# Differential attention on one core: the two maps are combined one tile further ahead, half on VectorE and half on GpSimd, with four buffers of scores

## The chip, the core and the metric

The kernel is one program on one core of a Trainium2 chip. Its engines are TensorE (PE), VectorE (DVE), ScalarE (ACT), GpSimd (POOL) and the queue that issues DMAs (SP). The metric is the time of one launch in device microseconds: the median of several runs, lower is better.

## What is computed

A two-layer decoder step: a gated linear attention layer, then a differential attention layer, both for a prompt of 2048 rows and for 64 sample rows. The change is in the prompt part of differential attention. There are 8 heads of 128 columns; each head has two maps of 64 columns:

```python
s = jnp.einsum('bqhmd,bkhmd->bhmqk', qs, ks).astype(F32) * (DIFF_DH ** -0.5)
s = s + bias[None, :, None]
s = jnp.where(rel >= 0, s, jnp.finfo(F32).min)
p = jax.nn.softmax(s, axis=-1)
a = p[:, :, 0] - lam * p[:, :, 1]
return jnp.einsum('bhqk,bkhd->bqhd', a, v.astype(F32))
```

## The kernel before

The phases run one after another with a barrier between them: projection, recurrence, residual, projection, prompt attention, sample attention, residual. Only `attention` is changed. It runs over 8 heads H and, in each, over T = 16 tiles i of 128 queries; tile i has i+1 blocks of 128 keys (the causal part). The loop over heads is unrolled by two; inside a head all 16 tiles are written out. Every engine has its own program of the same shape, and semaphores tie them together. No scheduler is involved: the order on each engine is the order in which the code is written.

What is done for tile i, by function:

- `scores` (PE, L1661 to L1665): for each piece of up to 512 keys and each of the two maps three matmuls into one of RING = 4 PSUM banks `ps_s`. Two maps of one piece of keys take two banks, called a chunk below: tiles 0 to 3 have one chunk, 4 to 7 two, 8 to 11 three, 12 to 15 four. The first chunk of a tile is the one that is cut short. A bank is written again only after `take` has read it (`piece_free`).
- `take` (DVE, L1819 and L1826): adds the bias, writes the scores to `s_sb` in SBUF and keeps the maxima; at its end L1834 and L1836 make the negated maximum `neg`.
- `exps` (ACT, L1741): the exponential of the whole row in place, once for each map m, with the row's sum into `total`.
- `combine` (DVE, L1844 to L1852): the reciprocals `inv`, a weight for the second map, and `a = s[1] * weight + s[0]` over all (i+1)*128 columns.
- `turn` (PE, L1678) transposes `a` in groups of four blocks into the banks `ps_a`; `copies` (ACT, L1753) moves a group to SBUF as `a_t`; `meet` (PE, L1692) multiplies it with v into `ps_o`; `output` (ACT, L1760) scales and writes the tile's result, and counts `o_copied`.
- `prep`, `high`, `low` (L1643, L1735, L1793 and L1796) prepare q and k of the next head, one eighth in every even tile.

In iteration i the engines do this: PE the scores of tile i+2, with turns and meets of tile i woven in after the second chunk; ACT `exps(i+1, 0)`, then the first two copies of tile i, then `exps(i+1, 1)`, the other copies, `output(i)`; DVE `take(i+1)`, then `combine(i)`. GpSimd does nothing in this phase.

Of the kernel before, what the change touches and what calls it, by code (L numbers as in the profile page):

```python
# [11 lines left out]
ALU = mybir.AluOpType  # L12
# [3 lines left out]
P = 128  # L16
# [36 lines left out]
class Core:  # L53


    def __init__(self, nc, ctx):
        self.nc, self.ctx, self.sems = nc, ctx, []

        self.passed = {e.engine: nc.alloc_semaphore(name=f"passed_{i}")
                       for i, e in enumerate((nc.vector, nc.tensor, nc.sync))}  # L60
# [1439 lines left out]
def attention(core, q, k, v, rev, rel_bias, o):  # L1500
# [14 lines left out]
    RING = 4  # L1515

# [3 lines left out]
    with ExitStack() as mem:  # L1520
# [3 lines left out]
        def ps(name):  # L1524
# [12 lines left out]
        s_sb = [sb(f"s{i}", [P, 2, SEQ]) for i in range(2)]  # L1537
# [7 lines left out]
        weight = sb("weight", [P, 1])  # L1545
# [11 lines left out]
              "weight_done a_done a_turned a_copied a_met o_copied").split()}  # L1557
# [4 lines left out]
        def ahead(H, u, i, by):  # L1562

            return (H, u, i + by) if i + by < T else (H + 1, 1 - u, i + by - T)

# [13 lines left out]
        with nc.Block() as block:  # L1579
# [53 lines left out]
            def _(pe):  # L1633
# [35 lines left out]
                def turn(H, i, g):  # L1669

                    if g == 0:
                        pe.wait_ge(s["a_done"], after(T * H + i + 1))
# [52 lines left out]
                for i in range(2):  # L1725
                    for _ in scores(0, 0, i):
                        pass
# [3 lines left out]
            def _(act):  # L1731
# [6 lines left out]
                def exps(H, u, i, m):  # L1738
                    n = (i + 1) * P
                    act.wait_ge(s["neg_done"], after(T * H + i + 1))  # L1740
                    nc.scalar.activation(s_sb[i % 2][:, m, 0:n], s_sb[i % 2][:, m, 0:n], ACT.Exp,  # L1741
                                         bias=neg[i % 2][:, m:m + 1],
                                         accum_out=total[i % 2][:, m:m + 1]).then_inc(s["exp_done"], 1)
# [40 lines left out]

            @block.vector
            def _(dve):
# [13 lines left out]
                def take(H, u, i):  # L1800
# [3 lines left out]
                    if not (isinstance(H, int) and H == 0 and i == 0):  # L1804

                        dve.wait_ge(s["a_done"], after(T * H + i - 1))
# [3 lines left out]
                    for c, (lo_, hi_) in enumerate(pieces[i]):  # L1810
                        cut, start = min(hi_, near), max(lo_, near)
                        for m in range(2):
# [5 lines left out]
                            if cut > lo_:  # L1818
                                ins = nc.vector.tensor_scalar(s_sb[i % 2][:, m, lo_:cut],  # L1819
# [3 lines left out]
                            if hi_ > near:  # L1823
                                if cut <= lo_:
                                    stand_alone(dve, core)
                                ins = nc.vector.tensor_tensor_reduce(  # L1826
                                    out=s_sb[i % 2][:, m, start:hi_], in0=ps_s[n % RING][:, start - lo_:hi_ - lo_],
# [10 lines left out]
                def combine(H, u, i):  # L1838
                    n = (i + 1) * P
                    dve.wait_ge(s["exp_done"], after(2 * (T * H + i + 1)))  # L1840
                    if i >= 2:

                        dve.wait_ge(s["o_copied"], after(T * H + i - 1))
# [3 lines left out]
                    nc.vector.scalar_tensor_tensor(weight[:, :], total[i % 2][:, 0:1], core.neg_lambda[:, :],  # L1847
# [3 lines left out]
                    dve.wait_ge(s["a_turned"], after(GROUPS * H + first_group[max(i - 1, 0)]))  # L1851
                    nc.vector.scalar_tensor_tensor(a[i % 2][:, 0:n], s_sb[i % 2][:, 1, 0:n], weight[:, :],  # L1852
                                                   s_sb[i % 2][:, 0, 0:n], ALU.mult, ALU.add).then_inc(s["a_done"], 1)
# [10 lines left out]
                dve.sem_inc(s["piece_free"], RING)  # L1864
                for n, (is_q, g) in enumerate(preps):
                    low(0, 0, n, is_q, g, turn_banks)
                take(0, 0, 0)
                over_heads(dve, head)
# [507 lines left out]
```

## Time and profile before

| | |
|---|---|
| median of 3 runs | 3785.05 us (3784.03 to 3786.7) |
| profiled execution, its time | 3788.77 us |
| its span | 3787.0 us |
| PE, DVE, ACT, POOL busy over the span | 3424.4, 1771.8, 1099.7, 118.9 us |
| mean granted TensorE clock | 0.959 |
| prompt attention | from about 2157 to 3022 us of the span |

Times in the profile are microseconds from the start of the span. "Idle before" stands for the time in which an engine stood still ahead of an instruction, and behind the arrow is what released it. A line such as `L1852` is a line of the kernel before. Busy times count overlapping instructions of an engine once.

### The profile page before, as it was taken

What the parts mean: (1) busy time and instruction counts of PE and PEld (TensorE: products, weight loads), DVE (VectorE), ACT (ScalarE), POOL (GpSimd) and SP (SyncE); (2) the same over time, 40 slices, a digit from 0 to 9 for tenths busy, and PEclk for the clock granted to TensorE, in tenths of its full rate; (3) what the DMA queues carried; (4) which work ended last, traced back from release to release, by engine and by line L of the source; (5) the groups of instructions that cost most, each with busy time, mean ns of one, the idle gap of its engine ahead of it and who ended that gap; (6) DMA issues with size and microseconds to landing.
All of it is one profiled execution on the core that took longest, in us unless ns stands there. A gap on an engine that the chain in (4) does not pass through costs nothing. (4 is left out here: it accounts for less than half of the span.)

```text
span 3787.0 us, 54465 instructions
## 1 busy us (share of the span) xinstructions
PE 3424.4 (90%) x19319; PEld 2764.8 (73%) x19319; DVE 1771.8 (47%) x4120; ACT 1099.7 (29%) x1875; POOL 118.9 (3%) x158
## 2 busy tenths in 40 slices
PE   9999997995999989999999888888888778589999
PEld 7888995773888868888888666666666645378887
DVE  2123113555555542111113388887888734455554
ACT  2111102332121212111111166666666522311111
POOL 0000002110000000000000000000000000000000
PEclk9999998997999999999999989999999988799999
DMA  4621213336222224122221311111110088622221
GB/s 169 87 79 64 81 48 103 116 103 227 87 78 84 77 78 137 70 73 73 77 78 60 93 43 46 41 46 41 45 40 12 15 316 311 232 85 76 89 76 48
DMA packets 199098, 350.72 MB, mean 93 GB/s; under 512 B 19005, under 2 KB 109918, under 8 KB 198894
## 3 DMA queue, kind: packets, MB, share of 16 engines
q1 hardware_dynamic: 198894, 348.04, 27.9%
q8 instruction: 123, 2.02, 0.2%
q14 instruction: 81, 0.66, 0.1%
HBM read 243.50 MB, written 104.47 MB: 92 GB/s over the span
## 5 line engine op out<-in xcount | busy, mean ns | idle before, releaser
L362 PE MATMUL in_ps_y<-in_w_hi,in_x_hi 128*128 128x512 f32 (+2 forms) x1920 | 725.3, 378 | 0.0
L366 PE MATMUL in_ps_y<-in_w_hi,in_x_lo 128*128 128x512 f32 (+2 forms) x1920 | 722.2, 376 | 0.0
L364 PE MATMUL in_ps_y<-in_w_lo,in_x_hi 128*128 128x512 f32 (+2 forms) x1920 | 722.1, 376 | 0.0
L366 PEld LDWEIGHTS in_ps_y<-in_w_hi,in_x_lo 128*128 128x128 f32 x1920 | 361.5, 188 | 60.4
L362 PEld LDWEIGHTS in_ps_y<-in_w_hi,in_x_hi 128*128 128x128 f32 x1920 | 361.8, 188 | 59.8 <-ACT in_out L437 0.6
L364 PEld LDWEIGHTS in_ps_y<-in_w_lo,in_x_hi 128*128 128x128 f32 x1920 | 361.7, 188 | 58.9
L506 DVE COPY in_out<-in_ps_y 128x512 f32<-128x512 f32 (+2 forms) x88 | 56.7, 645 | 686.2 <-PE in_ps_y L366 647.0
L1819 DVE TENSOR_SCALAR_CACHE_REDUCE att_s<-att_ps_s,att_far 128x256 f32<-128x256 f32 (+3 forms) x608 | 328.4, 582 | 43.5 <-PE att_ps_s L1665 35.4
L1692 PE MATMUL att_ps_o<-att_v,att_a_t 128*128 128x128 f32 x2176 | 305.6, 289 | 32.5 <-ACT att_a_t L1753 31.6
L1692 PEld LDWEIGHTS att_ps_o<-att_v,att_a_t 128*128 128x128 f32 x2176 | 268.7, 196 | 85.5 <-ACT att_a_t L1753 58.5
L1741 ACT ACTIVATE att_s<-att_s,att_neg 128x128 f32<-128x128 f32 (+15 forms) x256 | 306.8, 1199 | 7.7 <-DVE att_neg L1836 7.6
L437 ACT ACTIVATE in_out<-in_ps_y 128x512 f32<-128x512 f32 (+2 forms) x88 | 49.4, 561 | 678.7 <-PE in_ps_y L366 636.7
L1255 PE MATMUL res_ps_f<-res_w_hi,res_o_hi 128*128 128x512 f32 x544 | 221.1, 406 | 7.8 <-ACT res_w_hi L1367 7.8
L1678 PE MATMUL att_ps_a<-ident,att_a 128*128 128x128 f32 x1088 | 166.8, 284 | 66.5 <-DVE att_a L1852 65.4
L1255 PE MATMUL res_ps_g<-res_w_hi,res_h_hi 128*128 128x512 f32 x544 | 218.7, 402 | 3.9 <-issue 3.9
L1257 PE MATMUL res_ps_f<-res_w_lo,res_o_hi 128*128 128x512 f32 x544 | 217.9, 400 | 0.0
L1259 PE MATMUL res_ps_f<-res_w_hi,res_o_lo 128*128 128x512 f32 x544 | 217.6, 400 | 0.0
L1259 PE MATMUL res_ps_g<-res_w_hi,res_h_lo 128*128 128x512 f32 x544 | 215.8, 397 | 0.0
L1257 PE MATMUL res_ps_g<-res_w_lo,res_h_hi 128*128 128x512 f32 x544 | 215.7, 397 | 0.0
L1678 PEld LDWEIGHTS att_ps_a<-ident,att_a 128*128 128x128 f32 x1088 | 122.6, 143 | 118.3 <-DVE att_a L1852 107.6
L1753 ACT ACTIVATE att_a_t<-att_ps_a 128x512 f32<-128x512 f32 (+2 forms) x320 | 160.0, 532 | 152.4 <-PE att_ps_a L1678 151.4
L1852 DVE SCALAR_TENSOR_TENSOR att_a<-att_s,att_weight 128x128 f32<-128x128 f32 (+15 forms) x128 | 173.0, 1352 | 23.8 <-PE att_ps_a L1678 12.1
(256 smaller groups left out, 4792.4 us busy)
## 6 DMA issues: line engine op xcount, KB each, us to landing
smp_k_pg<-in_cache_k SPq DMA_DIRECT2D x64, 512.0 KB, 5.7
smp_v_pg<-in_cache_v SPq DMA_DIRECT2D x64, 512.0 KB
res_factors<-factors SPq DMA_DIRECT2D x34, 512.0 KB
res_o<-mixer_out SPq DMA_DIRECT2D x34, 512.0 KB, 4.5
factors<-in_out SPq DMA_DIRECT2D x64, 256.0 KB, 2.0
in_stage<-in_diff_w_in SPq DMA_DIRECT2D x16, 1024.0 KB, 8.5
gla_x<-gla_qka SPq DMA_DIRECT2D x17, 520.0 KB, 3.5
gla_v<-gla_v SPq DMA_DIRECT2D x17, 512.0 KB, 4.3
```

Of the source, the lines that this page charges most:

```text
L362: nc.tensor.matmul(bank[:, cols], x_hi[:, k, rows], w_hi[:, k, cols], start=(k == 0), stop=False)
L364: nc.tensor.matmul(bank[:, cols], x_hi[:, k, rows], w_lo[:, k, cols], start=False, stop=False)
L366: mm = nc.tensor.matmul(bank[:, cols], x_lo[:, k, rows], w_hi[:, k, cols], start=False, stop=(k == KD - 1))
L1255: nc.tensor.matmul(dst[:, cols], hi[kind][:, k, :], w_hi[n][:, k, cols], start=(k == 0), stop=False)
L1257: nc.tensor.matmul(dst[:, cols], hi[kind][:, k, :], w_lo[n][:, k, cols], start=False, stop=False)
L1259: mm = nc.tensor.matmul(dst[:, cols], lo[kind][:, k, :], w_hi[n][:, k, cols], start=False, stop=(k == K - 1))
L1678: mm = nc.tensor.transpose(ps_a[n % 2][:, (b % 4) * P:(b % 4 + 1) * P], a[i % 2][:, b * P:(b + 1) * P], core.ident[:, :])
L1692: mm = nc.tensor.matmul(ps_o[:, 0:D_VD], a_t[n % 2][:, (b % 4) * P:(b % 4 + 1) * P], v_sb[u][:, b, :], start=(b == 0), stop=(b == i))
L1741: nc.scalar.activation(s_sb[i % 2][:, m, 0:n], s_sb[i % 2][:, m, 0:n], ACT.Exp, bias=neg[i % 2][:, m:m + 1], accum_out=total[i % 2][:, m:m ...
L1753: nc.scalar.activation(a_t[n % 2][:, 0:cols], ps_a[n % 2][:, 0:cols], ACT.Copy).then_inc(s["a_copied"], 1)
L1819: ins = nc.vector.tensor_scalar(s_sb[i % 2][:, m, lo_:cut], ps_s[n % RING][:, 0:cut - lo_], far[u][:, :], None, ALU.add, ALU.max, accum_ou ...
L1852: nc.vector.scalar_tensor_tensor(a[i % 2][:, 0:n], s_sb[i % 2][:, 1, 0:n], weight[:, :], s_sb[i % 2][:, 0, 0:n], ALU.mult, ALU.add).then_i ...
```

## The change

`combine` is moved ahead by one tile on DVE: iteration i is now `take(i+2)`, then `combine(i+1)`, and `take(1)` and `combine(0)` stand ahead of the loop. PE's scores are made three tiles ahead instead of two (AHEAD = 3). There are four buffers `s_sb` instead of two, and two of `weight`. `combine` writes on DVE only the first i//2+1 blocks of `a` (`own`); the others are made on GpSimd by a `tensor_scalar` (times weight, in place) and a `tensor_tensor` (add). The program of ScalarE is the same except for the number of the buffer.

```diff
+    AHEAD, HELD = 3, 4
...
-        s_sb = [sb(f"s{i}", [P, 2, SEQ]) for i in range(2)]
+        s_sb = [sb(f"s{i}", [P, 2, SEQ]) for i in range(HELD)]
...
-                        if not (last and i + 2 >= T):
-                            ahead_to = ahead(H, u, i, 2)
+                        if not (last and i + AHEAD >= T):
+                            ahead_to = ahead(H, u, i, AHEAD)
...
+            @block.gpsimd
+            def _(pool):
+                def combine(H, u, i):
+
+                    cols = slice(own(i) * P, (i + 1) * P)
+                    if own(i) > i:
+                        return
+                    pool.wait_ge(s["weight_done"], after(T * H + i + 1))
+                    stand_alone(pool, core)
+                    nc.gpsimd.tensor_scalar(s_sb[i % HELD][:, 1, cols], s_sb[i % HELD][:, 1, cols],
+                                            weight[i % 2][:, :], None, ALU.mult).then_inc(s["a_weighed"], 1)
+                    wait_turned(pool, H, i)
+                    pool.wait_ge(s["a_weighed"], after(pooled(H, i)))
+                    nc.gpsimd.tensor_tensor(a[i % 2][:, cols], s_sb[i % HELD][:, 0, cols],
+                                            s_sb[i % HELD][:, 1, cols], ALU.add).then_inc(s["a_pooled"], 1)
...
                 def combine(H, u, i):
-                    n = (i + 1) * P
+                    n = own(i) * P
                     dve.wait_ge(s["exp_done"], after(2 * (T * H + i + 1)))
...
                 def head(H, u, last):
                     for i in range(T):
+                        if not (last and i + 2 >= T):
+                            take(*ahead(H, u, i, 2))
                         if not (last and i + 1 >= T):
-                            take(*ahead(H, u, i, 1))
-                        combine(H, u, i)
+                            combine(*ahead(H, u, i, 1))
```

DVE before, around the take of tile 14 (17 passes over 384, 512 and 256 columns, cut here) and the combination behind it; REGISTER_ALU and ISA rows are waits and counters:

```order
L1852 SCALAR_TENSOR_TENSOR att_a<-att_s,att_weight 128x1664
L1789 REGISTER_ALU
L1796 TENSOR_TENSOR att_k_lo<-att_ps_k,att_k_hi 128x512
L1814 REGISTER_ALU
L1819 TENSOR_SCALAR att_s,att_mx<-att_ps_s,att_far 128x384
...
L1834 TENSOR_REDUCE att_top<-att_mx 128x2
L1835 REGISTER_ALU
L1836 TENSOR_SCALAR att_neg<-att_top 128x2
L1840 ISA
L1844 RECIPROCAL att_inv<-att_total 128x2
L1847 SCALAR_TENSOR_TENSOR att_weight<-att_total,neg_lambda,att_inv 128x1
L1851 REGISTER_ALU
L1852 SCALAR_TENSOR_TENSOR att_a<-att_s,att_weight 128x1792
```

DVE with the change, at the same take of tile 14:

```order
L1897 SCALAR_TENSOR_TENSOR att_a<-att_s,att_weight 128x896
L1849 REGISTER_ALU
L1858 REGISTER_ALU
L1863 TENSOR_SCALAR att_s,att_mx<-att_ps_s,att_far 128x384
...
L1878 TENSOR_REDUCE att_top<-att_mx 128x2
L1880 TENSOR_SCALAR att_neg<-att_top 128x2
L1884 ISA
L1888 RECIPROCAL att_inv<-att_total 128x2
L1891 REGISTER_ALU
L1892 SCALAR_TENSOR_TENSOR att_weight<-att_total,neg_lambda,att_inv 128x1
L1570 REGISTER_ALU
L1897 SCALAR_TENSOR_TENSOR att_a<-att_s,att_weight 128x896
```

Ahead of the take stands the combination of tile 12 in both, and behind it the combination of tile 13: the takes and combinations of DVE alternate as before, only their iteration has another number. The `low` (L1796) that stood ahead of this take now stands behind the combination of tile 13, and the combination has 896 columns instead of 1792.

ACT with the change (before, the rows are the same but for the line numbers), from the output of tile 11 to the second exponential of tile 13:

```order
L1779 ACTIVATE att_o<-att_ps_o,att_inv 128x128
L1752 REGISTER_ALU
L1754 ACTIVATE att_k_hi<-att_ps_k 128x512
L1759 REGISTER_ALU
L1760 ACTIVATE att_s,att_total<-att_s,att_neg 128x1792
L1767 REGISTER_ALU
L1772 ACTIVATE att_a_t<-att_ps_a 128x512
L1767 REGISTER_ALU
L1772 ACTIVATE att_a_t<-att_ps_a 128x512
L1760 ACTIVATE att_s,att_total<-att_s,att_neg 128x1792
```

The second exponential of tile 13 stands behind the output of tile 11, the first exponential and the two copies of tile 12, now as before.

PE with the change, in iteration 12: the second chunk of the scores of tile 15, then the turns of tile 12, then the third chunk:

```order
L1674 REGISTER_ALU x2
L1677 MATMUL att_ps_s<-att_k_hi,att_q_hi 128x512 x2
L1679 MATMUL att_ps_s<-att_k_lo,att_q_hi 128x512 x2
L1681 MATMUL att_ps_s<-att_k_hi,att_q_lo 128x512 x2
L1688 REGISTER_ALU
L1697 MATMUL att_ps_a<-ident,att_a 128x128 x4
L1691 REGISTER_ALU
L1697 MATMUL att_ps_a<-ident,att_a 128x128 x4
L1674 REGISTER_ALU x2
L1677 MATMUL att_ps_s<-att_k_hi,att_q_hi 128x512 x2
L1679 MATMUL att_ps_s<-att_k_lo,att_q_hi 128x512 x2
L1681 MATMUL att_ps_s<-att_k_hi,att_q_lo 128x512 x2
```

Before, the turns of tile 12 stood behind the second chunk of tile 14; now they stand behind the second chunk of tile 15.

## Rows read from the trace of the kernel before

**Rows 1.** the attention stage as one window; columns us, busy us (instructions), clock, DMA

```profile
2176.50:3022.00 845.50, 721.25 (x5392) 563.90 (x5388) 698.51 (x2409) 541.34 (x1012) 0.00 (x0) 0.96 0.13 37
```

**Rows 2.** who waited for whom inside 2176.5 to 3022; total us, times, longest

```profile
PE att_ps_a L1678 <- DVE att_a L1852: 65.4, 82, 2.0
...
DVE att_s L1819 <- PE att_ps_s L1665: 35.4, 52, 2.2
...
DVE att_inv L1844 <- ACT att_s L1741: 25.9, 15, 3.9
DVE att_k_lo L1796 <- ACT att_k_hi L1735: 24.1, 9, 5.7
...
DVE att_s L1819 <- DVE att_a L1852: 7.3, 34, 0.2
```

**Rows 3.** costliest groups of the page, the two that this change touches

```profile
L1741 ACT ACTIVATE att_s<-att_s,att_neg 128x128 f32<-128x128 f32 (+15 forms) x256 | 306.8, 1199 | 7.7 <-DVE att_neg L1836 7.6
...
L1852 DVE SCALAR_TENSOR_TENSOR att_a<-att_s,att_weight 128x128 f32<-128x128 f32 (+15 forms) x128 | 173.0, 1352 | 23.8 <-PE att_ps_a L1678 12.1
```

**Rows 4.** timeline of one large tile; start us, duration us, what, [idle before]

```profile
2571.76 1.78 ACT L1741 ACTIVATE att_s<-att_s,att_neg 128x1792 f32<-128x1792 f32 x1
...
2573.85 0.61 DVE L1819 TENSOR_SCALAR_CACHE_REDUCE att_s<-att_ps_s,att_far 128x384 f32<-128x384 f32 x1
2574.08 1.08 ACT L1753 ACTIVATE att_a_t<-att_ps_a 128x512 f32<-128x512 f32 x2 [0.45 <-PE att_ps_a L1678]
...
2575.05 1.79 ACT L1741 ACTIVATE att_s<-att_s,att_neg 128x1792 f32<-128x1792 f32 x1
...
2575.06 0.50 PE L1661 MATMUL att_ps_s<-att_k_hi,att_q_hi 64*128 64x512 f32 x2 [0.58 <-DVE att_s L1819]
...
2579.47 1.28 PE L1692 MATMUL att_ps_o<-att_v,att_a_t 128*128 128x128 f32 x10
...
2580.47 0.17 DVE L1844 RECIPROCAL att_inv<-att_total 128x2 f32<-128x2 f32 x1
...
2580.87 0.37 ACT L1760 ACTIVATE att_o<-att_ps_o,att_inv 128x128 f32<-128x128 f32 x1 [0.92 <-PE att_ps_o L1692]
2581.01 2.08 DVE L1852 SCALAR_TENSOR_TENSOR att_a<-att_s,att_weight 128x1792 f32<-128x1792 f32 x1
```

**Rows 5.** timeline of two small tiles

```profile
2510.62 0.50 PE L1661 MATMUL att_ps_s<-att_k_hi,att_q_hi 64*128 64x512 f32 x2
...
2510.97 0.17 DVE L1844 RECIPROCAL att_inv<-att_total 128x2 f32<-128x2 f32 x1
...
2518.02 0.40 PE L1661 MATMUL att_ps_s<-att_k_hi,att_q_hi 64*128 64x512 f32 x2
...
2518.81 0.77 PE L1678 MATMUL att_ps_a<-ident,att_a 128*128 128x128 f32 x5
...
2520.16 0.94 ACT L1741 ACTIVATE att_s<-att_s,att_neg 128x768 f32<-128x768 f32 x1
```

**Rows 6.** timeline at the end of a head

```profile
2596.88 0.17 DVE L1844 RECIPROCAL att_inv<-att_total 128x2 f32<-128x2 f32 x1 [2.49 <-ACT att_s L1741]
```

**Rows 7.** timeline in the first layer, GpSimd and VectorE side by side

```profile
709.07 1.28 POOL L754 TENSOR_TENSOR gla_k_end<-gla_x,gla_e_rem 128x512 f32<-128x512 f32 x1 [8.70 <-ACT gla_e_rem L954]
...
709.72 1.17 DVE L1011 SCALAR_TENSOR_TENSOR gla_q_dec<-gla_x,gla_e_cum 128x512 f32<-128x512 f32 x1
...
711.82 0.69 DVE L1004 SCALAR_TENSOR_TENSOR gla_la<-gla_z,gla_za 128x512 f32<-128x512 f32 x1 [0.33 <-ACT gla_za L936]
```

**Rows 8.** GpSimd's groups, shapes kept apart

```profile
L754 POOL TENSOR_TENSOR gla_k_end<-gla_x,gla_e_rem 128x512 f32<-128x512 f32 x17 | 21.7, 1275 | 145.4 <-ACT gla_e_rem L954 145.4
...
L711 POOL MEMSET gla_q_one<- 128x2048 f32 x1 | 1.8, 1805 | 0.1
```

**Rows 9.** an idle TensorE and the clock behind it

```profile
2174.86 1.09 PE L1643 MATMUL att_ps_k<-ident,att_k_nat 128*128 128x128 f32 x4 [4.57 <-DMA att_q_nat<-diff_q]
...
2172.00:2196.00 24.00, 19.03 (x80) 0.52 0.57 138
```

More of the change, by code:

```diff
@@ L59, in __init__ @@
         self.passed = {e.engine: nc.alloc_semaphore(name=f"passed_{i}")
-                       for i, e in enumerate((nc.vector, nc.tensor, nc.sync))}
+                       for i, e in enumerate((nc.vector, nc.tensor, nc.sync, nc.gpsimd))}
     def sem(self, name):
@@ L1544, in attention @@
         inv = [sb(f"inv{i}", [P, 2]) for i in range(2)]
-        weight = sb("weight", [P, 1])
+        weight = [sb(f"weight{i}", [P, 1]) for i in range(2)]
         o_sb = [sb(f"o{i}", [P, D_VD]) for i in range(2)]
@@ L1564, in ahead, with wait_turned, own, pooled @@
             return (H, u, i + by) if i + by < T else (H + 1, 1 - u, i + by - T)
+        def wait_turned(eng, H, i):
+            if i >= 2:
+                eng.wait_ge(s["a_turned"], after(GROUPS * H + first_group[i - 1]))
+            elif not (isinstance(H, int) and H == 0):
+                eng.wait_ge(s["a_turned"], after(GROUPS * H - sum(groups[T - 1 + i:])))
+        def own(i):
+            return i // 2 + 1
+        def pooled(H, i):
+            return (T - 1) * H + (i if i >= 0 else i + 1)
         def over_heads(eng, head):
@@ L1671, in turn @@
                     if g == 0:
-                        pe.wait_ge(s["a_done"], after(T * H + i + 1))
+                        pe.wait_ge(s["a_done"], after(HELD + T * H + i + 1))
+                    if g == own(i) // 4 and own(i) <= i:
+                        pe.wait_ge(s["a_pooled"], after(HELD + pooled(H, i)))
                     n = first_group[i] + g
@@ L1724, in _ @@
                     prep(0, n, is_q, g, turn_banks)
-                for i in range(2):
+                for i in range(AHEAD):
                     for _ in scores(0, 0, i):
@@ L1740, in exps @@
                     act.wait_ge(s["neg_done"], after(T * H + i + 1))
-                    nc.scalar.activation(s_sb[i % 2][:, m, 0:n], s_sb[i % 2][:, m, 0:n], ACT.Exp,
+                    nc.scalar.activation(s_sb[i % HELD][:, m, 0:n], s_sb[i % HELD][:, m, 0:n], ACT.Exp,
                                          bias=neg[i % 2][:, m:m + 1],
@@ L1783, in _, with head @@
                 over_heads(act, head)
+            @block.gpsimd
[12 more added lines that the diff above has]
+                                            s_sb[i % HELD][:, 1, cols], ALU.add).then_inc(s["a_pooled"], 1)
+                def head(H, u, last):
+                    for i in range(T):
+                        if not (last and i + 1 >= T):
+                            combine(*ahead(H, u, i, 1))
+                pool.sem_inc(s["a_pooled"], HELD)
+                combine(0, 0, 0)
+                over_heads(pool, head)
             @block.vector
@@ L1803, in take @@
                         dve.wait_ge(head_in[u], after(48 * (H // 2 + 1) if isinstance(H, int) else 24 * (H - u) + 48))
-                    if not (isinstance(H, int) and H == 0 and i == 0):
-                        dve.wait_ge(s["a_done"], after(T * H + i - 1))
+                    dve.wait_ge(s["a_done"], after(T * H + i + 1))
+                    dve.wait_ge(s["a_pooled"], after(HELD + pooled(H, i - HELD)))
                     n_keys = (i + 1) * P
@@ L1838, in combine @@
                 def combine(H, u, i):
-                    n = (i + 1) * P
+                    n = own(i) * P
                     dve.wait_ge(s["exp_done"], after(2 * (T * H + i + 1)))
-                    if i >= 2:
+                    if not (isinstance(H, int) and H == 0 and i < 2):
                         dve.wait_ge(s["o_copied"], after(T * H + i - 1))
@@ L1845, in combine @@
                     dve.wait_ge(s["inv_done"], after(T * H + i + 1))
-                    nc.vector.scalar_tensor_tensor(weight[:, :], total[i % 2][:, 0:1], core.neg_lambda[:, :],
+                    dve.wait_ge(s["a_pooled"], after(HELD + pooled(H, i - 2)))
+                    nc.vector.scalar_tensor_tensor(weight[i % 2][:, :], total[i % 2][:, 0:1], core.neg_lambda[:, :],
                                                    inv[i % 2][:, 1:2], ALU.mult, ALU.mult).then_inc(s["weight_done"], 1)
                     dve.wait_ge(s["weight_done"], after(T * H + i + 1))
-                    dve.wait_ge(s["a_turned"], after(GROUPS * H + first_group[max(i - 1, 0)]))
-                    nc.vector.scalar_tensor_tensor(a[i % 2][:, 0:n], s_sb[i % 2][:, 1, 0:n], weight[:, :],
-                                                   s_sb[i % 2][:, 0, 0:n], ALU.mult, ALU.add).then_inc(s["a_done"], 1)
+                    wait_turned(dve, H, i)
+                    nc.vector.scalar_tensor_tensor(a[i % 2][:, 0:n], s_sb[i % HELD][:, 1, 0:n], weight[i % 2][:, :],
+                                                   s_sb[i % HELD][:, 0, 0:n], ALU.mult, ALU.add).then_inc(s["a_done"], 1)
                 def head(H, u, last):
                     for i in range(T):
+                        if not (last and i + 2 >= T):
+                            take(*ahead(H, u, i, 2))
                         if not (last and i + 1 >= T):
-                            take(*ahead(H, u, i, 1))
-                        combine(H, u, i)
+                            combine(*ahead(H, u, i, 1))
                         if not last:
@@ L1867, in _ @@
                 take(0, 0, 0)
+                take(0, 0, 1)
+                combine(0, 0, 0)
                 over_heads(dve, head)
```

7 lines of the change are left out of this document (4 added, 3 removed).

## The prediction

> **What bounds the kernel now.** I read the window of the attention stage first: of 845.5 us PE is busy for 721.3, DVE for 698.5, ACT for 541.3 and GpSimd for nothing [rows 1]; that is 106 us per head. No engine is full, so the stage is a chain that runs through several of them, and the table of waits says where. PE waits 65.4 us for the combined row, DVE 35.4 us for scores, and for exponentials only 25.9 us in 15 of 128 tiles [rows 2]. The last number matters most here. The exponentials are 307 us of ACT and are nearly always in time, and the combination is 173 us of DVE, 1.352 us on average [rows 3]. Both edits aim at DVE: shorter combinations, and PE not waiting for them. So the question is what the new order does to the exponentials' punctuality.
>
> In what follows k is the tile whose combination stands behind the take of tile k+1. This order of DVE is the same before and after. The second exponential of tile k stands on ACT behind the output of tile k-2, the first exponential of k and the two copies of tile k-1, and this is unchanged too. What changed is PE: the turns of tile k-1, for which these copies wait, stood behind the second chunk of the scores of tile k+1, and stand now behind the second chunk of tile k+2. With four banks, that chunk can be written only when `take(k+1)` has read its last bank.
>
> Before, then, turns, copies and second exponential ran **beside** `take(k+1)`. The large tile shows it: the take of tile 14 starts at 2573.85, the copies at 2574.08, the second exponential of tile 13 at 2575.05, and DVE's reciprocal comes without a wait at 2580.47 [rows 4]. With the change they come **after** the take, and DVE, whose next instruction is the combination of k, stands still. Nothing hides it: what is queued behind that reciprocal is take(k+2), for which PE's third chunk waits.
>
> **The wait for small tiles** (k = 2 to 6, at most two chunks in `take(k+1)`). PE begins its second chunk 0.35 us before the place of the reciprocal (2510.62 against 2510.97), the turns 0.79 later (2518.02 to 2518.81), the second exponential 1.35 after that (2520.16), and it takes 0.94 for 768 columns [rows 5], with 0.1 for reading the sum. For k = 5: 0.44 + 1.35 + 1.04 = 2.8 us. An exponential costs 0.105 us per 128 columns (0.94 at 768, 1.78 at 1792 [rows 4, 5]) and turns with copies 0.1 to 0.2 per block. That gives 1.9, 2.3, 2.6, 2.8 and 3.1 us: 12.7 per head.
>
> **The wait for large tiles** (k = 7 to 14, `take(k+1)` with three or four chunks). Here ACT comes late by another way: the output of tile k-2 needs the third chunk of tile k+1 first, and so the running take. For k = 13: the third chunk starts 1.21 us after the take (2575.06), and 6.18 us later the output of a tile of 13 blocks ended (2580.87 + 0.37 [rows 4]); now it is tile 11 with 12 blocks, 5.8. Output done at 7.0. Then one `high` in every second tile (0.6), the first exponential 1.78 + 0.1, two copies 0.97 (2574.08 to 2575.05), the second exponential 1.79 + 0.1: 12.3. The take is done after 6.62 (2580.47). Wait 5.7 us. In the same way, with the third chunk 0.7 to 1.5 us after the take's start by the length of the first chunk, the eight tiles give 3.7, 3.5, 4.6, 4.5, 4.4, 4.5, 5.6 and 5.5: 36.3 per head.
>
> **The sum.** Waits +49.0 us per head. The halved combination: a block of 128 columns costs (2.08 - 1.352)/(14 - 8.5) = 0.13 us [rows 3, 4]; 64 blocks per head go to GpSimd, 8.5 us per head or 68 in all, 48 of them in these tiles: -6.4. DVE waits that the new one swallows (for `low`'s input and the gap behind the combination, 24.1 + 7.3 us in the stage [rows 2], of which some 20 here): -2.5. From the combination of tile 14 to the fourth take of the next head the chain already goes through the exponentials of tile 15, with a wait of 2.49 us [rows 6]; the same working gives 21.2 instead of 20.5: +0.7. Together +40.8 per head, 326 for eight. The sum is made against the profiled time of 3788.8, which is 3.7 above the median shown; taken off, 4111.
>
> **GpSimd's part** costs nothing by itself. Its add takes at most 1.275 us for 512 columns, its scaling between 0.88 ns (a memset: 1.805 us for 2048) and 2.5 ns per column [rows 8]: at most 5.1 us for the largest pair of 1024 columns. PE needs the result behind the next take and the wait, over 10 us later. If that cover went, it would be those 5 us. The four buffers and second weight remove waits that do not bind: nothing. The extra register rows in `take` are tens of ns per tile: below 5 us in all.
>
> **The clock.** TensorE now stands still for 5 to 6 us of every 12 to 14 in the large tiles: from the turns until the third chunk. The trace has one gap of this size in the stage: 4.57 us idle, and the stretch around it ran at a granted clock of 0.52 although PE was busy for 19 of 24 us [rows 9], which is nearly its lower level, 1.2 of 2.4 GHz. At that level its parts of the chain double: about 4.3 us in each of 8 large tiles, 1.2 in each of 5 small ones, 10 at the head's end, 50 per head. So this costs between nothing and 400 us. I take half, 200, since each cycle also has 8 us of dense work. The Trainium skill ("TensorE: Matmul & The Clock Gate", Part 1) says that the array's clock is gated down when it has been idle and comes back under load; the row agrees, and by that rule the low level would recur in every large tile.
>
> 4111 + 200 gives **4310 us**.
>
> **Rivals.** (1) *ACT stays punctual and DVE bounds alone*: the halved combinations come off the stage, 68 us: 3717. For it: DVE is busy 83% of the stage and PE loses its wait of 65.4 us. Against it: the order rows; it would need copies of k-1 to be ready before the take ends. It decides where the new wait falls below what the halving saves, 0.53 us per tile; my smallest is 1.9. Chance 0.05. (2) *The change does nothing*: waits shift and cancel, 3785. It needs the added wait to be 0.5 to 0.6 us per tile. Chance 0.02. (3) *GpSimd holds DVE up as well.* In the first layer a two-input instruction of 512 columns on DVE took 1.17 us when it began beside GpSimd's multiply, and 0.69 without one; it ended 0.54 us after GpSimd's end [rows 7]. Both wait for the same weight here. If GpSimd wins the start in each tile, DVE's half waits for the scaling of up to 1024 columns: 8192 columns per head at 0.88 to 2.5 ns, 58 to 163 us in all, 4310 + 90 = 4400 nearer to the one-input end. If DVE wins, GpSimd waits, and nothing is lost. Chance 0.3. The Trainium skill ("SBUF — State Buffer", "SBUF: two separate sides") calls this an exclusive lock between GpSimd and a DVE instruction with two SBUF inputs, held for the whole instruction; the trace agrees. (4) *The forecast*: the new wait with a partly low clock and without that lock, 0.6. The remaining 0.03 are mistakes of mine in the slower direction.
>
> **How the numbers follow.** A measurement here tells changes over 0.2% from none. Slower: (3), (4) and the rest, 0.93; same 0.02; faster 0.05. The range runs from the sum without any clock loss, 4110, to 4490: clock loss nearly in full, or half of it with the lock at its upper price. Rivals 1 and 2 lie outside it with 0.07, and I leave about 0.1 more beyond its ends.
>
> **What the profile would show.** DVE's wait for exponentials (`att_inv` behind `att_s`) rises from 25.9 us to about 400 in over 100 tiles; the stage grows to 1170 to 1400 us; PE's wait for the combined row is nearly gone, and its gaps stand ahead of the third chunk, with `att_s` of DVE as releaser; the mean of DVE's combinations falls to about 0.85 us, or stays near 1.3 if rival 3 is at work; the granted clock of the stage falls from 0.96 to 0.7 or 0.8. I am wrong if the second exponential starts before the take ends, or if the chain's output on ACT comes much earlier than 7 us into a large take.

## The result: slower by 14%, and the profile after

The changed kernel takes 4327.48 us (4324.1 to 4330.85) against 3785.88 us (3784.03 to 3790.39) for the kernel before, a ratio of 1.1429 [1.1409, 1.1448]. The forecast was 4310.

The attention stage as one window of the changed kernel (columns as in [rows 1]):

```profile
2176.50:3564.00 1387.50, 930.34 (x5389) 719.79 (x5387) 637.92 (x2413) 535.93 (x1012) 432.20 (x240) 0.76 0.08 23
```

The whole loss is here: 1387.5 - 845.5 = 542.0 us [rows 1]. VectorE works 60.6 us less and PE, with the same instructions, is busy 209 us longer, because the granted clock fell from 0.96 to 0.76. Who waited for whom in this window, against [rows 2]:

```profile
DVE att_inv L1888 <- ACT att_s L1760: 594.6, 127, 7.3
ACT att_a_t L1772 <- PE att_ps_a L1697: 514.1, 144, 8.4
...
PE att_ps_s L1677 <- DVE att_s L1863: 357.3, 94, 6.4
ACT att_o L1779 <- PE att_ps_o L1711: 317.1, 128, 8.1
DVE att_s L1863 <- PE att_ps_s L1681: 101.9, 92, 3.0
...
PE att_ps_a L1697 <- POOL att_a L1817: 9.8, 8, 2.3
```

VectorE's wait for exponentials is now ahead of 127 of 128 combinations; in the kernel before it was 25.9 us. PE no longer waits for VectorE's combination; it waits for GpSimd's eight times. The table of waits is a circle: VectorE for ScalarE, ScalarE for PE, PE for VectorE. The timeline of the large tile k = 13 shows one turn of it, beside [rows 4]:

```profile
2823.30 0.61 DVE L1863 TENSOR_SCALAR_CACHE_REDUCE att_s<-att_ps_s,att_far 128x384 f32<-128x384 f32 x1
...
2824.52 0.80 PE L1677 MATMUL att_ps_s<-att_k_hi,att_q_hi 64*128 64x512 f32 x2 [5.29 <-DVE att_s L1863]
...
2831.21 0.17 DVE L1880 TENSOR_SCALAR att_neg<-att_top 128x2 f32<-128x2 f32 x1
2831.37 0.37 ACT L1779 ACTIVATE att_o<-att_ps_o,att_inv 128x128 f32<-128x128 f32 x1 [2.28 <-PE att_ps_o L1711]
2831.81 0.60 ACT L1754 ACTIVATE att_k_hi<-att_ps_k 128x512 fp32r<-128x512 f32 x1
2832.30 1.78 ACT L1760 ACTIVATE att_s<-att_s,att_neg 128x1792 f32<-128x1792 f32 x1
...
2833.29 1.09 PE L1697 MATMUL att_ps_a<-ident,att_a 128*128 128x128 f32 x8
...
2834.07 1.07 ACT L1772 ACTIVATE att_a_t<-att_ps_a 128x512 f32<-128x512 f32 x2
2835.03 1.79 ACT L1760 ACTIVATE att_s<-att_s,att_neg 128x1792 f32<-128x1792 f32 x1
...
2836.95 0.17 DVE L1888 RECIPROCAL att_inv<-att_total 128x2 f32<-128x2 f32 x1 [5.57 <-ACT att_s L1760]
...
2837.58 1.15 DVE L1897 SCALAR_TENSOR_TENSOR att_a<-att_s,att_weight 128x896 f32<-128x896 f32 x1
2837.66 3.46 POOL L1813 TENSOR_SCALAR att_s<-att_s,att_weight 128x896 f32<-128x896 f32 x1 [10.30 <-DVE att_weight L1892]
```

Read it from the take (2823.30): PE's third chunk comes 1.2 us later, after standing still for 5.29; the output of tile 11 starts only at 2831.37, as the take ends (its last instruction starts at 2831.21); then `high`, first exponential, copies, second exponential follow one another on ScalarE, and VectorE stands still all that time. Before, the same second exponential ended 3.6 us ahead of the reciprocal.

### The profile page after: what moved, and what is told of

Same layout as the page of the kernel before. It is cut to its first block and busy times, and to the rows that moved or that the text cites. A ratio compares the mean times of both kernels' runs of the same rounds, so it can differ in the third digit from the quotient of the medians.

```text
span 4329.1 us, 55591 instructions
## 1 busy us (share of the span) xinstructions
PE 3635.7 (84%) x19319; PEld 2922.2 (68%) x19319; DVE 1710.7 (40%) x4120; ACT 1093.8 (25%) x1875; POOL 551.0 (13%) x398
## 3 DMA queue, kind: packets, MB, share of 16 engines
q1 hardware_dynamic: 198894, 348.04, 24.1%
## 5 line engine op out<-in xcount | busy, mean ns | idle before, releaser
L1677 PE MATMUL att_ps_s<-att_k_hi,att_q_hi 64*128 64x512 f32 (+3 forms) x640 | 184.5, 571 | 392.0 <-DVE att_s L1863 357.3
L1813 POOL TENSOR_SCALAR att_s<-att_s,att_weight 128x128 f32<-128x128 f32 (+7 forms) x120 | 271.0, 2258 | 1712.5 <-DVE att_weight L1892 1712.5
L1711 PEld LDWEIGHTS att_ps_o<-att_v,att_a_t 128*128 128x128 f32 x2176 | 356.1, 251 | 129.5 <-issue 70.2
L1711 PE MATMUL att_ps_o<-att_v,att_a_t 128*128 128x128 f32 x2176 | 399.0, 347 | 51.0 <-ACT att_a_t L1772 49.6
L1677 PEld LDWEIGHTS att_ps_s<-att_k_hi,att_q_hi 64*128 64x128 f32 x640 | 76.4, 232 | 456.0 <-DVE att_s L1863 372.7
L1888 DVE RECIPROCAL att_inv<-att_total 128x2 f32<-128x2 f32 x128 | 21.2, 166 | 594.6 <-ACT att_s L1760 594.6
```

What stands on the lines that cost most here:

```text
L1677: nc.tensor.matmul(dst[m], q_hi[u][half, rows], k_hi[u][half, lo_:hi_], start=True, stop=False)
L1711: mm = nc.tensor.matmul(ps_o[:, 0:D_VD], a_t[n % 2][:, (b % 4) * P:(b % 4 + 1) * P], v_sb[u][:, b, :], start=(b == 0), stop=(b == i))
L1813: nc.gpsimd.tensor_scalar(s_sb[i % HELD][:, 1, cols], s_sb[i % HELD][:, 1, cols], weight[i % 2][:, :], None, ALU.mult).then_inc(s["a_weigh ...
```

## The experiments

Theory A is the forecast's: PE's new place for the turns, three tiles ahead with four banks, puts the second exponential behind the take; clock loss is a consequence. Rival B: GpSimd's half holds the chain up. Rival C: most of the loss is TensorE's clock. Every ratio below is against the kernel before, run on the same chip; "the table" is the one under e7.

**e1: exponentials one tile further ahead** (on ScalarE alone; its start and the end of its last head are fitted to it, cut here)

```diff
-                            exps(*ahead(H, u, i, 1), 0)
+                            exps(*ahead(H, u, i, 2), 0)
...
-                            exps(*ahead(H, u, i, 1), 1)
+                            exps(*ahead(H, u, i, 2), 1)
```

> The changed kernel with one edit: ScalarE makes both exponentials one tile further ahead (tile i+2 in iteration i instead of i+1). Theory A (order: the second exponential of the tile that VectorE combines next stands behind turns and an output that now come after the take): the new wait ahead of the reciprocal goes, since that exponential was made an iteration earlier; the stage falls from 1387 us to 800 to 870, its clock returns to above 0.9, the time is 3710 to 3800 us. Theory B (GpSimd's half is what holds the chain up): at most a tenth of the loss comes back, 4250 to 4330. Theory C (most of the loss is TensorE's low clock, set by its gaps): the gaps go with the waits, so this run does not tell C from A.

Measured 3766.37 us, ratio 0.9937 [0.992, 0.9953]: the loss is gone and the kernel is faster than before. Waits in its stage:

```profile
DVE att_inv L1889 <- ACT att_o L1779: 114.8, 73, 5.8
...
DVE att_s L1864 <- PE att_ps_s L1681: 23.9, 34, 0.9
```

VectorE waits no more for exponentials; what is left ahead of the reciprocal is the output of two tiles back. GpSimd works as in the changed kernel (271.1 us of scaling and 162.0 of adding, against 271.0 and 161.2), so rival B falls for the loss.

**The square e2, e3, e6.** e2 sets AHEAD = 2, e3 takes GpSimd out, e6 does both.

```diff
-    AHEAD, HELD = 3, 4
+    AHEAD, HELD = 2, 4
```

```diff
         def own(i):
 
-            return i // 2 + 1
+            return i + 1
...
-                combine(0, 0, 0)
-                over_heads(pool, head)
```

> The changed kernel with AHEAD = 2, as before the change; the split with GpSimd and the four buffers stay. PE, ScalarE and VectorE then have the order of the kernel before. Theory A: the second exponential runs beside the take again, VectorE's wait for exponentials is again below 50 us, and what is left is the split alone. If GpSimd's half is in time, 3720 to 3790 us. Theory B: the turns of a tile now stand right behind its combination, while GpSimd's scaling and add take 3.5 us on average (2.258 + 1.280 in the changed kernel), so PE waits for the add in most tiles, 1 to 2 us in each of 120, and the time is 3850 to 4000 us.

> The changed kernel with the whole combination on VectorE and nothing on GpSimd; everything else stays, scores three ahead too. Theory A: the order alone makes the loss; VectorE's combinations get 64 blocks of 0.13 us longer per head, all of it on the chain, so 4327 + 68 = 4395 us (4350 to 4420), with the wait of the reciprocal for exponentials still above 550 us. Theory B: without GpSimd the loss goes, 3790 to 3900.

> The changed kernel with both parts undone, scores two tiles ahead and nothing on GpSimd; four buffers, two weights and the added wait instructions stay. It is the fourth corner of a square: three ahead with GpSimd 4327, three ahead without 4343, two ahead with 4007. If the order explains all that GpSimd does not (theory A), this is the kernel before: 3780 to 3800. If the buffers or the extra instructions on the way to a take cost anything, it is above 3810.

| | with GpSimd | all on VectorE |
|---|---|---|
| scores three ahead | 4327.48 (1.1429) | 4343.5 (1.1469 [1.1449, 1.1488]) |
| scores two ahead | 4006.96 (1.0584 [1.0566, 1.0602]) | 3786.39 (0.9997 [0.9983, 1.001]) |

The lower right corner is as fast as the kernel before: four buffers, two weights and the added waits cost nothing that these runs can tell. Going up the right column is the order alone: 4343.5 - 3786.4 = 557 us. The bottom row says that the split by itself, in the old order, costs 221 us. There theory A's case for e2 missed and that of theory B came about, 7 us above the top of its range: rival B's mechanism is real. Waits of e2:

```profile
DVE att_s L1863 <- PE att_ps_s L1681: 302.8, 150, 8.5
...
PE att_ps_a L1697 <- POOL att_a L1817: 184.3, 95, 3.9
...
DVE att_inv L1888 <- ACT att_s L1760: 48.7, 36, 4.3
```

And one tile of e2 in its timeline:

```profile
2642.52 1.02 DVE L1897 SCALAR_TENSOR_TENSOR att_a<-att_s,att_weight 128x768 f32<-128x768 f32 x1
...
2642.60 2.68 POOL L1813 TENSOR_SCALAR att_s<-att_s,att_weight 128x640 f32<-128x640 f32 x1 [4.35 <-DVE att_weight L1892]
...
2645.37 1.53 POOL L1817 TENSOR_TENSOR att_a<-att_s 128x640 f32<-128x640 f32 x1
...
2646.95 0.76 PE L1697 MATMUL att_ps_a<-ident,att_a 128*128 128x128 f32 x4 [2.20 <-POOL att_a L1817]
```

GpSimd needs 4.3 us where VectorE's half took 1.02, and with scores two ahead the turns come right behind the combination. So the two parts of the change mask each other: the split needs the extra tile of distance, and the extra tile is what makes ScalarE late. This also shows how narrow "GpSimd's part costs nothing" was: it holds only because the turns had been moved.

In the new order the split saves just 16 us (e3 against the changed kernel), though VectorE's combinations are 68 us shorter. The expectation for e3 had put these 68 us on the chain in full, and its 4350 to 4420 missed. Their groups, first the changed kernel, then e3:

```profile
L1897 DVE SCALAR_TENSOR_TENSOR att_a<-att_s,att_weight 128x256 f32<-128x256 f32 (+7 forms) x128 | 104.7, 818 | 13.0
...
L1892 DVE SCALAR_TENSOR_TENSOR att_weight<-att_total,neg_lambda,att_inv 128x1 f32<-128x1 f32 x128 | 34.1, 266 | 12.4
```

```profile
L1893 DVE SCALAR_TENSOR_TENSOR att_a<-att_s,att_weight 128x128 f32<-128x128 f32 (+15 forms) x128 | 173.0, 1351 | 13.0
...
L1888 DVE SCALAR_TENSOR_TENSOR att_weight<-att_total,neg_lambda,att_inv 128x1 f32<-128x1 f32 x128 | 28.1, 219 | 4.5
...
L1885 DVE RECIPROCAL att_inv<-att_total 128x2 f32<-128x2 f32 x128 | 21.2, 166 | 561.7 <-ACT att_s L1760 561.7
```

The wait for exponentials is 33 us shorter in e3 (561.7 against 594.6): where ScalarE decides, a shorter combination only lengthens the wait. Another 14 us go to the weight, whose instructions are longer and have more idle time ahead in the changed kernel (34.1 + 12.4 against 28.1 + 4.5); where the 6 us of length come from is told under the rivals. The other 5 us are within what these runs can tell.

**e4: the clock alone.** PE does extra transposes whose result nobody reads; the order of the rest is untouched.

```diff
+                                if step == 2 and len(pieces[ahead_to[2]]) > 2:
+                                    pe.wait_ge(s["o_copied"], after(T * H + i))
+                                    spin(ps_o, 36)
...
+                        if 1 <= i <= 4:
+                            spin(ps_a[0], 14)
```

> The changed kernel with extra work on PE whose results nobody reads: 36 transposes of the identity (0.114 us each at full clock) between the turns and the third chunk of scores in the tiles with three or four chunks, and 14 at the end of iterations 1 to 4. They fill the gaps without touching the order of the rest. Theory A with the clock as the second term: the granted clock of the stage rises from 0.76 to above 0.9, PE's parts of the chain take their full-clock times, and 130 to 220 of the 542 us come back: 4110 to 4200. If the clock were the main term (theory C), more than 300 come back: below 4030. If the low clock costs nothing on the chain: 4320 to 4360.

Measured 4190.29 us, ratio 1.1066 [1.1047, 1.1084]: 137 us came back. Its stage:

```profile
2176.50:3426.00 1249.50, 1055.94 (x8144) 894.35 (x8142) 637.52 (x2418) 535.77 (x1016) 432.15 (x240) 0.94 0.09 26
```

And the group of the transposes that fill the large tiles:

```profile
L1687 PE MATMUL att_ps_o<-ident 128*128 128x128 f32 x2304 | 265.9, 275 | 0.0
```

PE did 266 us of extra work in these alone, and the kernel was faster for it. Rival C falls as the main cause: at a clock of 0.94, against 0.96 before, 404 us of loss remain (in the stage 1249.5 - 845.5 = 404.0). 137 is a lower bound for the clock's share, since the small tiles still ran at 0.82 to 0.91, but not far from it by an estimate from PE's own groups (all but the extra transposes): added up they are 897 us before, 1117 in the changed kernel and 914 in e4. e4 took back 203 of these 220 us, and what it left is at most some 17; this holds unless the transposes held the chain up themselves, which no run tells.

**e7 and e8: where PE's turns and meets stand.** e7 weaves the turns in behind the first chunk; e8 does all turns and meets of tile i before the scores of tile i+3.

```diff
-                                if 2 * step >= RING:
+                                if step >= 1:
```

```diff
                         mixed = values(H, u, i)
+                        for _ in mixed:
+                            pass
                         if not (last and i + AHEAD >= T):
```

> The changed kernel with PE's turns woven in behind the first chunk of the next scores instead of the second. Theory A says there are two ways to come late: small tiles wait for the turns behind the second chunk, large ones for the output behind the third and fourth chunk. This edit takes only the first away: the waits ahead of the reciprocal for k = 2 to 6 (2.9, 3.4, 3.8, 3.2, 4.3 us, mean of eight heads in the changed kernel) fall below 1 us, those for k = 7 to 14 (4.6 to 6.6 us) stay, so 100 to 140 us come back: 4190 to 4230. If the turns were what is late in large tiles too, 4000 or less.

> The changed kernel with PE doing all turns and meets of tile i before the scores of tile i+3, not woven in. Neither turns nor output of a tile then wait for the next take's banks. Theory A: exponentials are punctual again (DVE's wait for them below 150 us instead of 595), but PE makes scores later, so VectorE waits for scores more than before: 3750 to 3900 us. If the rest of the loss is in the clock or GpSimd, it stays above 4100.

e7: 4088.56 us, 1.0791 [1.0773, 1.0809]. e8: 3921.96 us, 1.0353 [1.0336, 1.0371]. The table adds up the waits ahead of the reciprocal, us per head, as means of the eight heads (in the kernel before 25.9/8 = 3.2, nearly all at the head's end). For the head's end the forecast gave no wait of its own, only +0.7 for a whole stretch:

| | k = 2 to 6 | k = 7 to 14 | k = 15, 0, 1 | granted clock of the stage |
|---|---|---|---|---|
| forecast, at full clock | 12.7 | 36.3 | | |
| changed kernel | 17.7 | 44.6 | 12.0 | 0.76 |
| e4 | 15.8 | 37.4 | 11.5 | 0.94 |
| e7 | 6.6 | 32.6 | 11.1 | 0.86 |
| e8 | 4.3 | 15.1 | 5.8 | 0.93 |

e7 took 11 us off the small tiles, as theory A has it, but only the first of them (k = 2) fell below 1 us, and the large ones fell by 12 us, which I had expected to stay; so 239 us came back where 100 to 140 were expected. Part of that can be the clock (e4's large tiles are 7.2 lower than the changed kernel's); the rest suggests that the turns were part of the delay in large tiles too, which no run shows by itself. e8 removes both causes and takes three quarters of the loss away, 22 us short of the range that I had given it, with 201.8 us of waits for exponentials where I expected under 150. Its rest has a new place: `high` now waits for `prep`, which stands behind all chunks on PE.

```profile
DVE att_inv L1885 <- ACT att_s L1757: 201.8, 113, 5.7
...
ACT att_k_hi L1751 <- PE att_ps_k L1659: 83.3, 28, 4.8
ACT att_q_hi L1751 <- PE att_ps_k L1659: 72.7, 28, 4.0
```

In the large tiles of e8 the wait is 1.9 to 3.3 us for the odd k, which have a `high` ahead of their exponentials, and 0.9 to 1.4 for the even ones.

**e12: GpSimd beside VectorE.** GpSimd's scaling waits for the end of VectorE's half.

```diff
-                    pool.wait_ge(s["weight_done"], after(T * H + i + 1))
+                    pool.wait_ge(s["a_done"], after(HELD + T * H + i + 1))
```

> The changed kernel with GpSimd's scaling waiting for the end of VectorE's half of the same tile (a_done) instead of for the weight. In the changed kernel the scaling of 896 columns is recorded from 0.08 us after the start of VectorE's instruction (1.15 us) and takes 3.46 us. If it stands still for as long as VectorE's two-input instruction runs and works only afterwards, it is recorded here with 2.4 us and ends at the same moment as before, and the time stays 4327 (within 10 us). If both really worked side by side, it takes 3.4 us here too and ends 1.1 us later, which the time does not show either, since PE waits for GpSimd only 9.8 us in all.

Measured 4333.01 us, 1.1444 [1.1422, 1.1466], the same as the changed kernel. GpSimd's groups by shape, the changed kernel's first, e12's second:

```profile
L1813 POOL TENSOR_SCALAR att_s<-att_s,att_weight 128x896 f32<-128x896 f32 x16 | 56.1, 3506 | 178.4 <-DVE att_weight L1892 178.4
...
L1817 POOL TENSOR_TENSOR att_a<-att_s 128x896 f32<-128x896 f32 x16 | 33.3, 2084 | 1.6 <-POOL att_s L1813 0.5 <-PE att_ps_a L1697 0.2
```

```profile
L1813 POOL TENSOR_SCALAR att_s<-att_s,att_weight 128x896 f32<-128x896 f32 x16 | 40.4, 2523 | 189.2 <-DVE att_a L1897 189.2
L1817 POOL TENSOR_TENSOR att_a<-att_s 128x896 f32<-128x896 f32 x16 | 33.3, 2083 | 1.6 <-POOL att_s L1813 0.6
```

The record is 0.98 us shorter, nearly the 1.07 us for which VectorE's instruction still ran after the old start. In the changed kernel, then, GpSimd did next to nothing while VectorE's two-input instruction ran, and VectorE, which began 0.08 us earlier, lost nothing (817 to 822 ns on average in every run with the half split). The scaling does not end at the same moment, as expected, but 0.34 us later in the mean of 16, since it starts 0.27 us after VectorE's end.

**Towards a faster kernel: e5, e9, e11, e13.** All have e1's exponentials. e5 takes GpSimd out; e9 gives `inv` four buffers, so that a combination waits for the output of four tiles back; e11 is e9 with fewer blocks on VectorE; e13 is e9 with e7's edit.

```diff
-        inv = [sb(f"inv{i}", [P, 2]) for i in range(2)]
+        inv = [sb(f"inv{i}", [P, 2]) for i in range(HELD)]
...
-                        dve.wait_ge(s["o_copied"], after(T * H + i - 1))
+                    dve.wait_ge(s["o_copied"], after(T * H + i + 1))
...
+                dve.sem_inc(s["o_copied"], HELD)
```

```diff
-            return i // 2 + 1
+            return max(1, 2 * (i + 1) // 5)
```

> e1 (exponentials one tile further ahead) with the whole combination on VectorE and nothing on GpSimd. VectorE's combinations are 68 us longer in the stage (173.0 against 104.7 in the trace of e3 and of e1). If VectorE's chain bounds e1 alone, 3766 + 68 = 3834 us. If e1 is bound by PE and ScalarE together (in e1 VectorE waits 114.8 us for outputs, which would swallow the longer combination), 3766 to 3790.

> e1 with four buffers of the reciprocals instead of two, so that the combination does not wait for the output of two tiles back (114.8 us, 73 times in e1). If that wait is on the chain, 30 to 100 us come off: 3670 to 3735. If it only stands in the shadow of PE, which is busy 714 of 824 us in e1's stage, VectorE waits as long for scores or exponentials instead: 3750 to 3770.

> e9 with a larger share for GpSimd: VectorE keeps 2(i+1)//5 blocks of tile i instead of i//2+1 (6 of 16 for the last tile instead of 8). 17 blocks per head go over, 0.1335 us each on VectorE: 18 us in all. If VectorE's chain bounds e9, 3731 us; if it is PE (busy 710 of 803 us), 3745 to 3750; if GpSimd, which needs some 7 us for the ten blocks of the last tile, is late for the turns, over 3760 with a wait of PE for GpSimd's add.

> e9 with PE's turns behind the first chunk of the next scores instead of the second. With exponentials a tile ahead nothing on VectorE waits for the turns any more; what could gain is ScalarE's chain copies, output (PE waits 41 us for copies, ScalarE 145 us for meets). If that chain is hidden, 3740 to 3755; if the earlier turns let the rest run closer, 3700 to 3740; if the turns now wait for GpSimd's add, over 3760.

| | us | ratio |
|---|---|---|
| e5 | 3824.87 | 1.0103 [1.0086, 1.012] |
| e1 | 3766.37 | 0.9937 [0.992, 0.9953] |
| e9 | 3749.24 | 0.9899 [0.9882, 0.9915] |
| e11 | 3730.74 | 0.9856 [0.9836, 0.9876] |
| e13 | 3768.92 | 0.9953 [0.9934, 0.9972] |

All but e5 are faster than the kernel before, by 0.5 to 1.4%. With punctual exponentials the split is worth 58.5 us (e1 against e5) of the 68 that it takes off VectorE. e9 took only 17 of the 114.8 us of waits for outputs: the wait stood mostly in the shadow of other work. e11 gave 18.5 us and came out at the 3731 that its expectation had for VectorE's chain as the bound of e9, but that is luck in part. It hands over 22 blocks per head, not the 17 counted there, and VectorE's combinations fell by 21.9 us in the traces, from 105.2 to 83.3. Against that, small instructions of VectorE at the ends of the heads became longer: the weights from 38.0 to 53.1 us (the lines below, e9 first, then e11), the negated maxima from 22.5 to 45.9. Fourteen of each kind start while GpSimd is at work and end with its instruction, as in the pair of e11's timeline that follows the weights:

```profile
L1891 DVE SCALAR_TENSOR_TENSOR att_weight<-att_total,neg_lambda,att_inv 128x1 f32<-128x1 f32 x128 | 38.0, 297 | 12.4
L1891 DVE SCALAR_TENSOR_TENSOR att_weight<-att_total,neg_lambda,att_inv 128x1 f32<-128x1 f32 x127 | 53.1, 418 | 12.5
```

```profile
2255.99 4.00 POOL L1814 TENSOR_SCALAR att_s<-att_s,att_weight 128x1152 f32<-128x1152 f32 x1 [2.31 <-DVE att_weight L1891]
2257.57 2.44 DVE L1881 TENSOR_SCALAR att_neg<-att_top 128x2 f32<-128x2 f32 x1
```

VectorE's busy time thus rose in the stage, from 638.3 to 653.1 us, and the time fell all the same: part of the longer instructions took the place of waits for exponentials (28.0 us in e9, 13.1 in e11). That VectorE's chain bounds e9 fits these numbers, but is not shown by them. e11's stage, and the two waits of PE that bear on it:

```profile
2176.50:2954.00 777.50, 698.45 (x5344) 549.14 (x5342) 653.11 (x2410) 536.27 (x1008) 514.16 (x240) 0.97 0.15 40
```

```profile
PE att_ps_o L1711 <- ACT att_a_t L1772: 41.8, 71, 2.1
...
PE att_ps_s L1677 <- DVE att_s L1864: 24.9, 51, 0.8
```

No wait for GpSimd's add stands among its waits, although GpSimd now works 514 us; PE is busy 90% of the window. e13 lost 20 us against e9, but not through GpSimd's add, as its expectation had it for this case, since no wait for it stands in the table: PE waits 82.2 us for copies instead of 41.3 and VectorE 58.7 us for scores instead of 35.4. A reason may be that the copies stand behind the first exponential on ScalarE however early the turns come; no run shows it. e11 is the fastest of all.

## Why the prediction was right

**The mechanism** held in each of its steps: the changed kernel waits for exponentials in 127 tiles (594.6 us, where I had about 400), PE's gaps moved ahead of the third chunk with VectorE's `att_s` as releaser, the output with which ScalarE's chain starts begins 8.1 us into the take and is done after 8.4 (forecast 7.0 at full clock), and the wait at k = 13 is 5.57 us (forecast 5.7). At the low clock both ends of that wait came later than forecast, the take's (8.1 us for 6.62) as well as the second exponential's (13.5 for 12.3), so the 5.57 is no test of either alone; e4, at 0.97 to 0.99 in its large tiles, has 5.51. e1 shows the cause: with the exponentials made earlier and all else the same the loss is gone. The square shows that the order alone gives it.

**The terms.** Two sizes were off and nearly cancel: the order at full clock, 326 forecast and 404 measured by e4 (78 short), and the clock, 200 taken and 137 measured (63 over). That the forecast came within 18 us of the time is luck in this respect: either miss alone would have put it 60 to 80 us off.
- The order. Cut VectorE's program into two stretches per head. From the combination of tile 14 to the fourth take of the next head it takes 20.4 us before, 24.1 in the changed kernel and 24.2 in e4 (means of seven): +3.8, where +0.7 was taken. The step that failed is "the same working gives 21.2 instead of 20.5": the waits for exponentials at k = 15, 0 and 1 grew by 11.5 - 3.2 = 8.3 us in e4, at k = 1 from nothing to 4.4, so the new place of the turns holds for these tiles too. The rest of the head grew from 85.9 to 132.7 us in e4 (means of six), +46.8 where 49.0 - 6.4 - 2.5 = +40.1 was taken. The waits in it are 53.2 instead of 49.0: the small tiles 15.8 against 12.7, at a clock of 0.82 to 0.91, the large ones 37.4 against 36.3. And the -2.5 was put in the wrong stretch: of the 24.1 us of waits for `low`'s input that the new one swallows, 21.4 stood at the heads' ends, as this one of the kernel before. The two stretches together are 9.8 us per head more than forecast, which is the 78.

```profile
2395.03 0.69 DVE L1796 TENSOR_TENSOR att_k_lo<-att_ps_k,att_k_hi 128x512 fp32r<-128x512 f32 x1 [5.68 <-ACT att_k_hi L1735]
```

- The clock: 200 taken, 137 measured as a lower bound. All of it came off the rest of the head (149.7 us in the changed kernel, 132.7 in e4); at the head's end, where 10 of my 50 us per head stood, 24.1 and 24.2 are the same. In the changed kernel the clock went up and down in each large tile, as these windows around one turn show (columns as above, the clock third from the end):

```profile
2819.20:2824.50 5.30, 0.03 (x1) 0.00 (x0) 2.65 (x8) 2.37 (x4) 2.18 (x1) 0.98 0.00 0
2824.50:2827.50 3.00, 2.98 (x12) 2.24 (x13) 2.61 (x7) 0.00 (x0) 2.78 (x2) 0.50 0.00 0
2828.00:2834.40 6.40, 6.38 (x51) 4.86 (x48) 1.92 (x10) 3.56 (x6) 0.00 (x0) 1.00 0.13 37
2834.40:2837.90 3.50, 0.00 (x0) 0.00 (x0) 0.71 (x3) 2.51 (x4) 0.24 (x1) 1.00 0.35 105
2838.00:2840.70 2.70, 0.00 (x0) 0.00 (x0) 2.70 (x7) 0.00 (x0) 2.70 (x1) 0.50 0.01 3
2840.70:2844.70 4.00, 3.98 (x17) 3.24 (x18) 2.74 (x8) 0.00 (x0) 2.51 (x2) 0.50 0.00 0
```

  The clock fell late in PE's idle stretch, at the end of the first one and 3.5 us into the second, and the low level (0.50) lasted into the work behind it. So the third chunk and the first meets pay, which are on the chain, and the eight turns ahead of the idle stretch (2833.29, 1.09 us) do not. That the low level would recur in every large tile, as the prediction drew from the Trainium skill's page "TensorE: Matmul & The Clock Gate", Part 1, agrees: in windows of 1 us over a whole head of the changed kernel it came back, to 0.50, behind each of the large tiles' idle stretches (2735 to 2855). The small tiles ran between 0.50 and 1.00, 0.54 to 0.73 in the mean of a head's small tiles.
- The halved combination: it stood in the sum with 51 us as if it came off the chain in full. In the sum that comes out (+53.2 of waits and -6.4 are the +46.8 measured), since VectorE does work less, but the edit is not worth that: without it (e3) the kernel is only 16 us slower, because the waits shrink instead.

**Rivals.** Rival 3 did not come about in the combinations: on VectorE they have a mean of 0.818 us and GpSimd waits instead, as "if DVE wins" had it. But the same thing happened to another instruction. The weight of tile 0 reads two small tiles in SBUF and has one column; at the end of each of seven heads it started beside GpSimd's add of tile 15 and ended with it, 0.38 to 1.61 us long instead of 0.22. The changed kernel's:

```profile
2867.64 2.35 POOL L1817 TENSOR_TENSOR att_a<-att_s 128x1024 f32<-128x1024 f32 x1
...
2868.39 1.61 DVE L1892 SCALAR_TENSOR_TENSOR att_weight<-att_total,neg_lambda,att_inv 128x1 f32<-128x1 f32 x1
```

These are the 6 us by which the weights are longer than in e3, 7.6 us of records where 1.5 would do. In e12, whose GpSimd is later, all seven take 1.92 to 1.95 us, and in e11, with its larger share for GpSimd, fourteen have a mean of 2.02 us. GpSimd's scaling was at the upper end of its bounds (2.5 ns per column), its add as in [rows 8]; the pair of 1024 columns takes 3.89 + 2.35 = 6.2 us, above my 5.1, because of the 1.1 us in which it stands still.

**Left open:** the share of the clock above 137 us, small by the estimate under e4; what besides the clock made e7's large tiles shorter; what bounds e9; and why e13 lost.

## What to carry to other kernels

When work is moved a tile ahead on one engine, look for the instruction on every other engine that the moved work now needs earlier, and move that too: here one edit on ScalarE turned 14% slower into 0.6% faster. How far ahead PE may make scores is set by the banks, not by the loop: with four of them "three ahead" put the last chunks, and all that was woven in behind them, after the take. Two parts of a change should be timed apart in all four corners: here each alone was slower (1.147 and 1.058), and neither number says what they do together or with the third edit.

## What the hardware showed unexpectedly

- Useless work can pay: extra transposes on PE in its idle stretches, 266 us of them in the large tiles, raised the stage's clock from 0.76 to 0.94 and took 137 us off.
- GpSimd's scaling of one tensor is slower per column than its add of two: 2.50 ns ((2.844 - 0.603)/896 from e12's shapes of 1024 and 128 columns, 8 and 16 records) against 2.10 ns ((2.338 - 0.455)/896). The Trainium skill ("GPSIMD Engine Reference", 4.1 Engine selection) calls a one-input operation roughly line-rate; for a scaling by a value per partition this case shows otherwise.
- A GpSimd instruction that stands still behind VectorE's two-input instruction is recorded as running: 3.51 us for 2.52 us of work. A record's length is no price before one knows what ran beside it.
- The other way round VectorE stands still. The weight, an instruction of one column with two inputs in SBUF, started beside GpSimd's add 41 times in the changed kernel, e9, e11 and e12, and 41 times it ended with the add, within 0.03 us. The reciprocal just ahead of it kept its 0.17 us beside the same add in the changed kernel. The negated maximum, with one input, was held beside GpSimd's scaling in all of 14 cases in e11 and in none of 14 in the changed kernel; why is open. In e11 the two cost VectorE 25 and 24 us, at the ends of the heads, where GpSimd's instructions are longest. No run here gives GpSimd less of the last two tiles alone.
